# A running sum, two squares, first chunks and layer-norm sums reordered in a three-layer fp32 network on one core

## The reference, cut to what matters

```python
def first_block(x, c, ctx, c_ctx, ada_w, ada_b, norm_gains, mlp_w_in, mlp_w_out, ...):
    ...
        a_lat = modulate(rmsnorm(h_lat, g_pre), mod_lat[0], mod_lat[1])
        ...
            y_lat = short_gated_conv(a_lat, sc_w_in[j], sc_conv[j], sc_w_out[j])
        ...
        h_lat = h_lat + mod_lat[2] * rmsnorm(y_lat.astype(h_lat.dtype), g_post)
        ...
        f_lat = squared_relu_mlp(modulate(rmsnorm(h_lat, g_pre_ff), mod_lat[3], mod_lat[4]), mlp_w_in[i], mlp_w_out[i])
        h_lat = h_lat + mod_lat[5] * rmsnorm(f_lat.astype(h_lat.dtype), g_post_ff)
...
def forgetting_attention(q, k, v, f_logit, q_g, k_g):
    ...
    c = jnp.cumsum(jax.nn.log_sigmoid(f_logit.astype(jnp.float32)), axis=1)
    ...
        s = s + cq_blk[..., :, None] - c_k[:, :, None, :]
...
def conformer_conv(h, w_pw1, dw_w, dw_b, ln_g, ln_b, w_pw2):
    a, g = jnp.split(h @ w_pw1, 2, axis=-1)
    u = a * jax.nn.sigmoid(g)
    u = causal_dwconv(u, dw_w, dw_b)
    u = jax.nn.silu(layer_norm(u, ln_g, ln_b))
    ...
def second_block(x, ...):
    for layer in range(DEPTH_2):
        ...
        if layer % 2 == 0:
            h = rms_norm(x, even_norm_g[i])
            x = x + even_mixer(h, ...)     # attention and pooling, then w_out
        else:
            h = rms_norm(x, odd_norm_g[i])
            x = x + conformer_conv(h, ...)
        h = rms_norm(x, ffn_norm_g[layer])
        x = x + conv_ffn(h, ffn_w_up[layer], ffn_conv_w[layer], ffn_conv_b[layer], ffn_w_down[layer])
    return x
```

## Time and profile before

| | us |
|---|---|
| median of three runs | 1751.17 (1751.17 to 1754.03) |
| the profiled execution: time | 1751.21 |
| the profiled execution: span | 1749.4 |
| PE busy | 1713.1 (98%) |
| DVE busy | 1088.5 (62%) |
| ACT busy | 691.4 (40%) |
| POOL busy | 150.3 (9%) |

### The profile page before, as it was taken

How to read it: one execution, slowest core, us unless ns; L and a number is a source line. 1 busy time by engine, 2 the same in 40 slices (tenths; PEclk the granted TensorE clock), 3 DMA queues, 4 the chain that set the end, 5 groups by cost and what they waited for, 6 DMA issues and landing times.

```text
span 1749.4 us, 21556 instructions
## 1 busy us (share of the span) xinstructions
PE 1713.1 (98%) x7720; PEld 1383.4 (79%) x7720; DVE 1088.5 (62%) x1660; ACT 691.4 (40%) x1005; POOL 150.3 (9%) x141
## 2 busy tenths in 40 slices
PE   8999999999999979999999999999989999999999
PEld 7888878888888768887888888877655788888888
DVE  6799884343434553746663663669997666366364
ACT  4322362222223423745432432447665543243242
POOL 0000400000000030000000000005892000000000
PEclk9999999999999989999999999999999999999999
DMA  8576414232323023103222222232210223223222
GB/s 284 186 240 223 135 50 134 94 102 93 120 95 99 25 72 98 49 1 97 96 96 96 96 96 96 84 108 72 72 49 24 96 96 99 94 96 101 91 84 85
DMA packets 182338, 176.22 MB, mean 101 GB/s; under 512 B 3304, under 2 KB 181740, under 8 KB 182268
## 3 DMA queue, kind: packets, MB, share of 16 engines
q1 hardware_dynamic: 182268, 175.29, 31.4%
HBM read 173.15 MB, written 2.10 MB: 100 GB/s over the span
## 4 chain that ended last, share of the span: by engine, by line
PE 87%; DVE 9%; issue 2%; ACT 1%; DMA 1%; SPq 0%; DVEq 0%; ACTq 0%
PE PSUM L1519 23%; PE PSUM L1521 23%; PE PSUM L1520 23%; DVE PSUM L1451 3%; DVE WL L945 1%; PE PSUM L1799 1%; PE PSUM L1781 1%; PE PSUM L1536 1%; PE PSUM L1824 1%; PE PSUM L1538 1%; PE PSUM L1826 1%; PE PSUM L1825 1%; PE PSUM L1537 1%; PE PSUM L1621 1%; PE PSUM L1937 1%
## 5 line engine op out<-in xcount | busy, mean ns | idle before, releaser
L562 ACT ACTIVATE WH<-RAW 128x1024 fp32r<-128x1024 f32 x274 | 281.5, 1052 | 731.6 <-PE PSUM L1521 704.1
L1519 PE MATMUL PSUM<-XH,WH 128*128 128x512 f32 x1152 | 451.5, 392 | 10.8 <-issue 10.8
L1521 PE MATMUL PSUM<-XH,WL 128*128 128x512 f32 x1152 | 449.2, 390 | 0.0
L1520 PE MATMUL PSUM<-XL,WH 128*128 128x512 f32 x1152 | 449.1, 390 | 0.0
L945 DVE TENSOR_TENSOR WL<-RAW,WH 128x1024 fp32r<-128x1024 f32 x274 | 339.9, 1263 | 10.5 <-ACT WH L562 10.5
L1519 PEld LDWEIGHTS PSUM<-XH,WH 128*128 128x128 f32 x1152 | 216.9, 188 | 56.6 <-issue 12.0
L1520 PEld LDWEIGHTS PSUM<-XL,WH 128*128 128x128 f32 x1152 | 216.9, 188 | 46.4 <-issue 1.2
L1519 PE MATMUL PSUM<-HH,WH 128*128 128x512 f32 x644 | 251.3, 390 | 1.8 <-issue 1.4
L1521 PEld LDWEIGHTS PSUM<-XH,WL 128*128 128x128 f32 x1152 | 216.8, 188 | 45.5
L1521 PE MATMUL PSUM<-HH,WL 128*128 128x512 f32 x644 | 250.6, 389 | 0.0
L1520 PE MATMUL PSUM<-HL,WH 128*128 128x512 f32 x644 | 250.6, 389 | 0.0
(11 more groups left out here) (311 smaller groups left out, 1998.4 us busy)
## 6 DMA issues: line engine op xcount, KB each, us to landing
RAW<-in_ffn_w_up SPq DMA_DIRECT2D x44, 1024.0 KB, 5.0
ARAW<-in_ada_w SPq DMA_DIRECT2D x24, 1024.0 KB, 5.3
RAW<-in_mlp_w_in SPq DMA_DIRECT2D x16, 1024.0 KB, 5.3
RAW<-in_mlp_w_out SPq DMA_DIRECT2D x16, 1024.0 KB, 5.0
RAW<-in_ffn_w_down SPq DMA_DIRECT2D x16, 1024.0 KB, 5.0
RAW<-in_sc_w_in SPq DMA_DIRECT2D x9, 1024.0 KB, 5.1
RAW<-in_even_w_in SPq DMA_DIRECT2D x8, 1024.0 KB, 5.6
RAW<-in_odd_w_pw SPq DMA_DIRECT2D x16, 512.0 KB, 5.2
```

The source lines that it names most:

```text
L562: act.activation(WH[:, j, a:b, :], RAW[:, j, a:b, :], ACT.Copy).then_inc(s_hi, 1)
L1519: pe.matmul(o, wh, mh[:, k, :], start=(k == 0), stop=False)
L1520: pe.matmul(o, wh, ml[:, k, :], start=False, stop=False)
L1521: mm = pe.matmul(o, wl, mh[:, k, :], start=False, stop=(k == kn - 1))
```

## The change

Six edits. **Running sum:** DVE's log decays and the nine additions no longer stand ahead of its windows; the decays stand in window 0 behind its evictions, the additions in threes at the ends of windows 0, 1 and 2, and the copy of the turned root at the end of window 1. **V:** in window 7 DVE copies row blocks 0 and 1, ACT blocks 2 and 3, and PE waits for these at step 3 of the attention. **Output projections:** in the first window of `U_EOUT` and `U_PW2`, ACT and DVE make the weight halves of unit u+2 before the split of the two chunks. **Two squares by PE** also for `ST_X3`; two fillers there go. **First chunks:** PE multiplies the high half of the first chunk by both weight halves as soon as the high half is there, and adds low x high after the wait for the low half. **Taps and sums:** in the last chunk PE has 10 taps instead of 12, ACT and Pool 8 instead of 7, DVE 13 instead of 12; DVE turns to the last unit one tap earlier; six of the eight layer-norm sums stand between PE's sixth and seventh tap.

The diff, cut to its core (left out: the calls of the same helpers at the start and at the MLP):

```diff
-TAPS_PE = (0, 3, 4, 4, 4, 5, 9, 12)
-TAPS_ADD = (10, 10, 10, 10, 10, 10, 9, 7)
-TAPS_EARLY = 10
+TAPS_PE = (0, 3, 4, 4, 4, 5, 9, 10)
+TAPS_ADD = (10, 10, 10, 10, 10, 10, 9, 8)
+TAPS_EARLY = (10, 10, 10, 10, 10, 10, 9)
+TAPS_AHEAD = 6
...
+TWO_BY_PE = (ST_Y0, ST_Y1, ST_X3)
...
-    return 9 * (stat - sum(other < stat for other in SUMMED_BY_PE)) - 2 * (stat > ST_Y0) - 2 * (stat > ST_Y1)
+    return 9 * (stat - sum(other < stat for other in SUMMED_BY_PE)) - 2 * sum(other < stat for other in TWO_BY_PE)
...
+            act.wait_ge(s_rc, 1)
+            act.wait_ge(s_mm, U_EVEN + 8)
+            for b in (2, 3):
+                act.activation(V[:, b, UW:2 * UW], PS_[:, 3, b % 2 * UW:b % 2 * UW + UW], ACT.Copy, scale=sc_(S_RT + b)
+                               ).then_inc(s_vr, 1)
             for s in range(4 * HEADS + 2):
...
+                first = u in (U_EOUT, U_PW2)
+                if first:
+                    hi_half(u + 2, 0, 0)
+                    hi_half(u + 2, 0, 1)
                 for c in range(2):
                     split_unscaled(stat, n + c, gain, k)
                     square(stat, n + c, X[:, n + c, :])
-                hi_half(u + 2, u % 2, 0)
-                hi_half(u + 2, u % 2, 1)
+                if not first:
+                    hi_half(u + 2, u % 2, 0)
+                    hi_half(u + 2, u % 2, 1)
...
+                    if n == 0:
+                        lo_half(u + 2, j, 0)
+                        lo_half(u + 2, j, 1)
+                        prep = False
                     for c in range(2):
                         lo_unscaled(stat, n + c, gain, k)
                         add_square(stat, n + c)
                 if prep and not (stat is not None and n == 6 and gain is None):
...
-                if stat is not None and gain is None and not (stat == ST_Y1 and n == 6):
+                if stat is not None and gain is None and not (stat in TWO_BY_PE and n == 6):
                     add_square(stat, n)
                     add_square(stat, n + 1)
...
-            dve.wait_ge(s_rt, 1)
-            dve.tensor_copy(sc_(S_RT, TB), PS_[:, ST_BANK, 0:TB]).then_inc(s_rc, 1)
-            dve.wait_ge(e_a, 3)
-
-            stt(TF[0:8, 1, :], CA[:, 1, 0:T], 0.0, CA[:, 0, 0:T], ALU.min, ALU.subtract).then_inc(e_c, 1)
-            dve.wait_ge(e_c, 1)
-            dve.memset(CA[:, :, 0:256], 0.0)
-            dve.tensor_copy(CA[:, 0, 256:256 + T], TF[0:8, 1, :]).then_inc(e_c, 1)
-            for n in range(9):
-                dve.wait_ge(e_c, n + 2)
-                a, b = n % 2, (n + 1) % 2
-                tt(CA[:, b, 256:256 + T], CA[:, a, 256:256 + T], CA[:, a, 256 - 2 ** n:256 + T - 2 ** n], ALU.add
-                   ).then_inc(e_c, 1)
+
+            def log_decays():
+
+                dve.wait_ge(e_a, 3)
+                stt(TF[0:8, 1, :], CA[:, 1, 0:T], 0.0, CA[:, 0, 0:T], ALU.min, ALU.subtract).then_inc(e_c, 1)
+                dve.wait_ge(e_c, 1)
+                dve.memset(CA[:, :, 0:256], 0.0)
+                dve.tensor_copy(CA[:, 0, 256:256 + T], TF[0:8, 1, :]).then_inc(e_c, 1)
+
+            def running_sum(p):
+
+                for n in range(3 * p, 3 * p + 3):
+                    dve.wait_ge(e_c, n + 2)
+                    a, b = n % 2, (n + 1) % 2
+                    tt(CA[:, b, 256:256 + T], CA[:, a, 256:256 + T], CA[:, a, 256 - 2 ** n:256 + T - 2 ** n], ALU.add
+                       ).then_inc(e_c, 1)
+
...
                     dve.tensor_copy(sc_(S_DUMP), sc_(S_EPS)).then_inc(s_ev, 1)
+                    if p == 0:
+                        log_decays()
...
-                    for b in range(TB):
+                    for b in range(TB if p == 6 else 2):
...
                     lo_half(u + 2, j, 0)
                     lo_half(u + 2, j, 1)
+                if p < 3:
+                    running_sum(p)
+                if p == 1:
+                    dve.wait_ge(s_rt, 1)
+                    dve.tensor_copy(sc_(S_RT, TB), PS_[:, ST_BANK, 0:TB]).then_inc(s_rc, 1)
...
-                    if tap == TAPS_EARLY and n + 1 < DC:
+                    if n + 1 < DC and tap == TAPS_EARLY[n]:
...
+            def first_chunk(u, units, mh, ml, base_, s_hi_chunk, hi):
+
+                pe.wait_ge(s_hi_chunk, hi)
+                for j in units:
+                    pe.wait_ge(s_lo, halves(u + j, 1))
+                    for c in range(2):
+                        wh, wl = (w[:, j, 0, c * P:c * P + P] for w in (WH, WL))
+                        pe.matmul(PS_[:, 2 * j + c, :], wh, mh[:, 0, :], start=True, stop=False)
+                        pe.matmul(PS_[:, 2 * j + c, :], wl, mh[:, 0, :], start=False, stop=False)
+                pe.wait_ge(s_x, base_ + 1)
+                for j in units:
+                    for c in range(2):
+                        pe.matmul(PS_[:, 2 * j + c, :], WH[:, j, 0, c * P:c * P + P], ml[:, 0, :], start=False, stop=False)
+
+            def two_units(u, mh, ml, base_, s_hi_chunk, hi):
 
                 pe.wait_ge(s_ev, u)
-                for first, last, units in ((0, 5, (0, 1)), (5, 8, (0,)), (5, 8, (1,))):
+                first_chunk(u, (0, 1), mh, ml, base_, s_hi_chunk, hi)
+                for first, last, units in ((1, 5, (0, 1)), (5, 8, (0,)), (5, 8, (1,))):
...
+            def first_chunk_of_x():
+
+                pe.wait_ge(sp_h, 1)
+                for u in range(FIRST):
+                    pe.wait_ge(s_lo0, pieces(0, u))
+                    raw, hi, lo = first_unit(u, 0)
+                    for c in range(2):
+                        o = PS_[:, (0, 2, 6)[u] + c, :]
+                        pe.matmul(o, hi[:, 0, c * P:c * P + P], XH[:, 0, :], start=True, stop=False)
+                        pe.matmul(o, lo[:, 0, c * P:c * P + P], XH[:, 0, :], start=False, stop=False)
+                pe.wait_ge(s_x, 1)
+                for u in range(FIRST):
+                    raw, hi, lo = first_unit(u, 0)
+                    for c in range(2):
+                        pe.matmul(PS_[:, (0, 2, 6)[u] + c, :], hi[:, 0, c * P:c * P + P], XL[:, 0, :], start=False, stop=False)
+                    shift_products(1, (0, 6, 11)[u], (6, 11, 16)[u])
...
+                if k == 0:
+                    pe.wait_ge(sp_g, 1)
+                    pe.matmul(o, FH[:, 0, :], XH[:, 0, :], start=True, stop=False)
+                    pe.matmul(o, FL[:, 0, :], XH[:, 0, :], start=False, stop=False)
+                    first_chunk(U_EVEN, (0,), XH, XL, 16, sp_g, 1)
+                    pe.matmul(o, FH[:, 0, :], XL[:, 0, :], start=False, stop=False)
+                else:
+                    if k == 4:
+                        pe.wait_ge(s_lo, halves(U_EVEN, 2))
+                    pe.wait_ge(s_x, 16 + k + 1)
+                    pe.matmul(o, FH[:, k, :], XH[:, k, :], start=False, stop=False)
+                    pe.matmul(o, FH[:, k, :], XL[:, k, :], start=False, stop=False)
+                    mm = pe.matmul(o, FL[:, k, :], XH[:, k, :], start=False, stop=(k == 7))
...
+                if s == 3:
+                    pe.wait_ge(s_vr, 2)
...
-            keep_busy(2)
-            channel_sum(ST_X3)
+            pe.wait_ge(s_r, ST_X3)
+            last_squares(ST_X3, ST_BANK)
+            two_squares(ST_X3, ST_BANK)
             keep_busy(3)
+            def chunk_sums(n):
+
+                pe.wait_ge(g_x, n + 1)
+                mm = pe.matmul(PS_[:, SUM_BANK, :], ONES[:, :], CV[:, n, :], start=False, stop=(n == DC - 1))
+                if n == DC - 1:
+                    mm.then_inc(n_1, 1)
+                pe.wait_ge(n_q, n + 1)
+                pe.matmul(PS_[:, SQUARE_BANK, :], ONES[:, :], TA[:, n % 2, :], start=False, stop=(n == DC - 1)
+                          ).then_inc(n_s, 1)
+
+            def first_sums():
+
+                pe.wait_ge(g_x, DC - 1)
+                pe.wait_ge(n_p, POOL_SUMS)
+                pe.matmul(PS_[:, SUM_BANK, :], ONES[:, :], SQ[:, :], start=True, stop=False)
+                pe.wait_ge(n_b, POOL_SUMS)
+                pe.matmul(PS_[:, SQUARE_BANK, :], ONES[:, :], SQS[:, :], start=True, stop=False)
+                for n in range(POOL_SUMS + 1, DC - 1):
+                    chunk_sums(n)
+
...
+                    if n == DC - 1 and k == TAPS_AHEAD:
+                        first_sums()
...
+                if n == 0:
+                    first_chunk(u, (0,), XH, XL, 40, sp_h, 16 + 1)
+                for k in range(1 if n == 0 else 0, 8):
...
-            pe.wait_ge(g_x, DC - 1)
-            pe.wait_ge(n_p, POOL_SUMS)
-            pe.matmul(PS_[:, SUM_BANK, :], ONES[:, :], SQ[:, :], start=True, stop=False)
-            pe.wait_ge(n_b, POOL_SUMS)
-            pe.matmul(PS_[:, SQUARE_BANK, :], ONES[:, :], SQS[:, :], start=True, stop=False)
-            for n in range(POOL_SUMS + 1, DC):
-                pe.wait_ge(g_x, n + 1)
-                mm = pe.matmul(PS_[:, SUM_BANK, :], ONES[:, :], CV[:, n, :], start=False, stop=(n == DC - 1))
-                if n == DC - 1:
-                    mm.then_inc(n_1, 1)
```

(46 more changed lines are left out.)

19 lines of the change are left out of this document (10 added, 9 removed).

## The result

The changed kernel takes 1731.97 us (median of four runs, 1731.85 to 1733.58), the kernel before 1752.6 in the runs beside it; the ratio is 0.9884, 95% interval 0.9867 to 0.9901. The profiled execution took 1731.89, with a span of 1730.1, against 1751.21 and 1749.4: 19.3 us less, where 21.6 were forecast (1729.6). The place of the missing 2.3 us is plain if one follows the same event through both traces, stage by stage. The table was made so: the start of one event in each trace, the difference, and what the difference gained since the row above.

The account below looks back on a forecast made before the run. PE bounds the kernel, with few short waits and one long one of 10.8 us. Terms 13.5 + 0.8 + 2.5 + 0.7 + 0.9 + 3.2 = 21.6 off 1751.2 give 1729.6; own range 1727.5 to 1732, stated range 1726.5 to 1736.

Parts of the forecast that it names:

- part 5: First chunks, high halves first: 0.5 us gained at the start, 0.4 at the even norm, 0 at the MLP's norm.
- if the clock is at 0.50 in a place where it wasn't: Sign that the prediction is wrong: PE's clock at 1.2 GHz in a place where it was not before.
- V 0.5 and the last junction 1.2 less: Upward margin of the forecast's own range: V's eviction gains 0.5 us less, the last taps' junction 1.2 less.
- Part 1: Running sum behind the first even units: removes PE's 10.8 us wait and 2.8 of low clock, 13.5 us.
- Parts 2 to 4: V's last eviction half on ACT 0.8 us; output projections' weight halves first 2.5; two squares by PE at ST_X3 0.7.
- Part 3: Output projections' first windows: weight halves ahead of the split remove waits of 1.1 and 1.4 us, 2.5 together.
- The first rival: Clock falls elsewhere, at ST_X3 or around the last taps: one fall costs 1.8 to 2.8 us, 1731.5 to 1734; chance 0.18.
- Part 6: Last conformer chunk, layer-norm sums among PE's taps: 3.2 us in all, with no clock fall in the taps.
- The race that was called the closest: Last conformer chunk: PE's taps end 0.1 us ahead of DVE's wait for them.
- The second rival: Pool's sums beside the second and third even windows slow DVE, PE waits 1 to 4 us: 1731 to 1734; chance 0.07.
- The last two: Rivals: ACT's third step late, PE waits as before, 1743, chance 0.03; low clock in dense 590 to 713, 1767, chance 0.05.

Follow-up runs that it names:

- gap_fill: Kernel before, with eleven filler products of PE put into its 10.8 us rest before the third even unit; 1748.77 us, ratio 0.9981.
- start_by_unit: Changed kernel with the very first chunk's high products first but unit by unit (4 high, 2 low, then small ones); 1731.14 us, run again 1729.56.
- columns_early: Changed kernel with the old first-chunk order and the 32 128x1 modulation-column products moved some 25 us earlier, between two dense units; 1736.39 us.
- start_spread: Changed kernel with the first chunk's high products still first, each unit's 128x1 products put behind its four high products; 1732.01 us, ratio 0.9888.
- start_old: Changed kernel with the old order of the very first chunk (high, low and weight low half of each product together); 1729.49 us, ratio 0.9872.
- pool_late: Changed kernel with the old first-chunk order, Pool's window sums held until the running sum's last addition; 1730.22 us, ratio 0.9872.

## Why the prediction was right, and where it was not

The time of 1731.97 lies within the stated range, and even within the forecast's own 1727.5 to 1732, by 0.03. That it does is partly luck, because one step failed (part 5, below) and by one of the prediction's own signs it was wrong: "if the clock is at 0.50 in a place where it wasn't". Where the range reached up to 1732, it was for other reasons: V 0.5 and the last junction 1.2 less.

**Part 1** (13.5, measured 13.4) was right in each term: gap_fill puts the low clock at 2.6 (forecast 2.8), the rest is the other 10.8. The steps of the path came as worked out: `log_decays` began at 621.10, right behind ACT's third step, and the low halves ended at 622.63 + 2.33 = 625.0, 3 us ahead of PE's need at 628.2.

**Parts 2 to 4** (0.8, 2.5, 0.7; measured 0.8, 2.9, 0.8): the waits went as a whole. Part 3 was a little short because I took only the wait for its size: EOUT gave 1.3 where the wait was 1.1, PW2 1.6 to 1.7 where it was 1.4. Behind such a wait the second product also starts late (793.64 to 793.98 and 1360.04 to 1360.35, where 0.23 is usual), which makes 0.1 of it; the rest I can't place.

**Part 5** is where it failed. The sentence "It adds no matmul, only order" is true and was taken to mean that the order can only gain. At the start the first product did begin 0.7 earlier; but the order also took the full-width products from between the 128x1 ones, and the clock fell for 6.8 us: from -0.7 at the first product the difference went to +2.4, so the fall cost 3.2, where the prediction has a gain of 0.5 and no cost. I had looked for a fall only behind idle time ("the rows show the lower clock only behind idle time or tiny products") and had searched for idles, at ST_X3 and around the last taps, not for tiny products, although the same sentence named them. The first rival, "the clock falls elsewhere", came true in a place that it did not name (it had ST_X3 and the last taps), behind small products and not behind an idle, and larger than it said: 3.2 for one fall, where it had 1.8 to 2.8. The time lies in that rival's 1731.5 to 1734; it is 2.3 over the forecast and not 3.2, because the earlier start gave 0.2 more than forecast and the other steps 0.6 to 0.7 more. With the old order the kernel measures 1729.5, which looks like the forecast of 1729.6 but isn't: without the 0.5 of the start the forecast's sum is 1730.1, and the same 0.6 make up the difference. The kernel that has the earlier start and no fall (start_by_unit) takes 1728.6 to 1728.9 in its lowest runs. At the even norm the step gave 0.6 for 0.4, at the MLP 0 as said.

The Trainium skill, page "TensorE: Matmul & The Clock Gate", section "HAM oscillation — how this bites in real kernels", puts the return to half rate down to idle gaps of PE. At 34.6 and at 199.4 there is none: the trace differs, and the trace decides.

**Part 6** (3.2, measured 3.3) was right in the sum and partly for a reason that I had not separated. The forecast subtracted from a trace whose taps ran partly at 0.50; the fall comes in 3 of 5 such traces, so 1.7 of the 3.3 is a gain only against an execution that had it. That part 6 takes the fall away (none in 9 traces) is what the prediction said, and for the reason that it gave, the shorter idle; that it is the idle and not the number or order of the taps is not shown. The race that was called the closest was won: the last plain product ended at 1310.8, 0.3 ahead of the addition at 1311.11.

**The second rival** (Pool holds DVE) had the mechanism and 2.4 us of extra time on the triple where 1.9 for each addition was feared; slack of 6.2 covered it. Its sum was also too small by its own terms: the pair of 4.1 and three additions of 2.6 are 11.9, and the eviction of 1.3, which belongs to the window too, makes them 13.2; measured were 9.9 (627.33 to 632.75 + 4.46). **The last two** left no trace: ACT's third step was in time, and PE ran at 1.00 from 590 to 703.

**A version that beats both**: the changed kernel with the first chunk's high products first unit by unit. In eight runs its lowest are 1728.61, 1728.68 and 1728.92, against 1731.83 to 1731.89 for the three lowest of the changed kernel's eight; the medians are 1731.14 and 1731.97 in the first set, 1729.56 and 1732.59 in the second. Its step is shown in three traces of ungathered orders (0.7 to 0.8 each).

## What to carry to other kernels

Before reordering work on an engine whose clock depends on what it does, list not only its waits but also which instructions stand between its cheap ones: moving the wide ones together can cost more than the wait that it removes, at 100% busy. When a forecast subtracts a low clock seen in one trace, look whether a second trace has it; a gain that rests on it is a gain of that execution. And small work that stands in a junction which another engine ends was free there, and cost its full length where PE is dense (3.6 us).

## What the runs showed of the hardware

- The clock fell to 0.50 (1.2 GHz) at 100% busy of PE, behind 22 to 32 products of 128x1 with none to four full-width ones among them (at 34.6, 35.8 and 36.3 in the gathered order, at 199.5 in columns_early), and not where groups of 10 to 12 of them alternate with four (start_spread) or six (start_by_unit, start_old) of full width.
- Ahead of the last taps, an idle of 2.2 was followed by a fall in 3 traces of 5, one of 1.5 in none of 9.
- In half of the traces the clock fell once between 18 and 28 us, for 1.5 to 3.5 of cost, whatever the kernel: steps of that size between runs of one kernel can come from there.
- Pool's and DVE's instructions with two SBUF inputs slow each other: DVE's low half 2.35 to 4.10 a pair, its 8x512 addition 0.70 to 1.49, Pool's addition over 527 columns 1.07 beside DVE's memsets (pool_late) and 1.93 beside DVE's low halves. Beside Pool's 128x1 instructions (from 643.88 on in the changed kernel) three additions took 2.10, as alone.
